# PEER expert stage: expert buffers of four slots by a quarter tile, added through four column groups of TensorE

## The reference, cut to what matters

```
s1, s2  = scores of the query's halves against 128 keys each
v1, i1  = top_k(s1, 16); v2, i2 = top_k(s2, 16)
w, p    = top_k(v1[:, None] + v2[None, :], 16)
expert  = i1[p // 16] * 128 + i2[p % 16]
y      += softmax(w) * gelu(dot(u[expert], h2)) @ v[expert]
```

## Time and profile before

| | |
|---|---|
| median of 3 runs | 1576.5 us (1575.19 to 1578.99) |
| profiled execution, its own time | 1576.8 us |
| its span, first to last instruction | 1575.5 us |
| mean granted clock of PE | 0.906 |
| busy: PE, DVE, ACT, POOL | 1310.1, 969.3, 283.7, 303.1 us |
| HBM read | 381.60 MB |

### The profile page before, as it was taken

How to read it: one execution, slowest core, us unless ns; L and a number is a source line. 1 busy time by engine, 2 the same in 40 slices (tenths; PEclk the granted TensorE clock), 3 DMA queues, 4 the chain that set the end, 5 groups by cost and what they waited for, 6 DMA issues and landing times.

```text
span 1575.5 us, 13461 instructions
## 1 busy us (share of the span) xinstructions
PE 1310.1 (83%) x4409; PEld 751.7 (48%) x4409; DVE 969.3 (62%) x2619; ACT 283.7 (18%) x642; POOL 303.1 (19%) x260
## 2 busy tenths in 40 slices
PE   7997999998899769998768739787878879696887
PEld 4766655676755336444454514333333435252333
DVE  5486533278453245541224789797969797888755
ACT  2014322102322211242221211111101010101000
POOL 0000000000000000000000044444544535354550
PEclk9998999999899769999658969898998989899999
DMA  7542453363153051053000199999999999999995
GB/s 280 189 148 107 160 173 137 107 218 143 54 214 107 32 195 56 32 208 142 1 0 1 61 415 426 425 426 424 426 424 427 423 415 424 419 418 415 422 427 244
DMA packets 105560, 384.58 MB, mean 244 GB/s; under 512 B 10763, under 2 KB 33854, under 8 KB 72722
## 3 DMA queue, kind: packets, MB, share of 16 engines
q0 software_dynamic: 36864, 268.45, 40.6%
q1 hardware_dynamic: 68626, 115.27, 20.6%
HBM read 381.60 MB, written 1.05 MB: 243 GB/s over the span
## 4 chain that ended last, share of the span: by engine, by line
PE 28%; DMA 17%; DVE 15%; issue 2%; ACT 2%; POOL 1%; DVEq 0%; SPq 0%; ACTq 0%
PE bank L174 27%; DMA e_uv<-in_experts_dram,e_chosen 17%; DVE e_uv L2459 3%; DVE e_hot L190 1%; DVE e_diag L196 1%; POOL e_uv L2583 1%; DVE second_hT L197 1%; DVE ml_W L190 1%; PE bank L179 1%; DVE e_e L215 1%; ACT m_sq L234 1%; DMA m_fin_g<-in_final_g_dram 0%; DVE m_fin_g L202 0%; ACT m_ctx L238 0%; DVE e_part L196 0%
## 5 line engine op out<-in xcount | busy, mean ns | idle before, releaser
L174 PE MATMUL bank<-e_uv,e_diag 128*128 128x512 f32 x1024 | 478.7, 625 | 133.7 <-DVE e_diag L196 133.6
L2583 POOL DMA_INDIRECT e_uv<-in_experts_dram,e_chosen x256 | 302.9, 1183 | 1231.7 <-DVE e_chosen L207 900.4
L174 PEld LDWEIGHTS bank<-e_uv,e_diag 128*128 128x128 f32 x1024 | 200.8, 200 | 400.5 <-issue 257.6
L2459 DVE CUSTOM_DVE_ANT_0 e_uv<-e_uv,second_h 128x1024 f32<-128x1024 f32 x256 | 305.0, 1222 | 99.5 <-DMA e_uv<-in_experts_dram,e_chosen 99.4
L174 PE MATMUL bank<-hT,weights 128*128 128x256 f32 x640 | 149.8, 397 | 10.4 <-DVE fb L202 8.8
L174 PEld LDWEIGHTS bank<-hT,weights 128*128 128x128 f32 x640 | 127.0, 200 | 29.7 <-DVE fb L202 8.9
L174 PE MATMUL bank<-weights,hT 128*128 128x512 f32 (+1 forms) x256 | 102.0, 555 | 2.0 <-DMA weights<-in_w_in_dram 2.0
L234 ACT ACTIVATE e_act<-e_dot 128x4 f32<-128x4 f32 (+1 forms) x67 | 13.7, 205 | 487.7 <-DVE e_dot L2459 487.7
L202 DVE SCALAR_TENSOR_TENSOR conv<-ubuf,vec,conv 128x256 f32<-128x256 f32 x240 | 96.8, 480 | 0.6
L174 PE MATMUL bank<-weights,mixT 128*128 128x512 f32 x192 | 91.1, 630 | 1.8 <-DVE mixT L207 1.6
L174 PE MATMUL bank<-m_w,second_hT 128*128 128x512 f32 (+1 forms) x160 | 70.3, 598 | 3.3 <-DVE second_hT L197 1.9
(11 more groups left out here) (350 smaller groups left out, 1326.3 us busy)
## 6 DMA issues: line engine op xcount, KB each, us to landing
weights<-in_w_in_dram SPq DMA_DIRECT2D x16, 2048.0 KB, 7.7
weights<-in_w_ada_dram SPq DMA_DIRECT2D x8, 2048.0 KB, 7.7
weights<-in_w_out_dram SPq DMA_DIRECT2D x6, 2048.0 KB, 7.6
weights<-in_cmp_w_dram SPq DMA_DIRECT2D x4, 2048.0 KB, 8.0
m_w<-in_w_ada_dram SPq DMA_DIRECT2D x4, 2048.0 KB, 8.3
e_w_pq<-in_w_pq_dram SPq DMA_DIRECT2D x8, 1024.0 KB, 24.4
m_w<-in_w_in_dram SPq DMA_DIRECT2D x3, 2048.0 KB, 14.0
m_w<-in_w_out_dram SPq DMA_DIRECT2D x2, 2048.0 KB, 8.7
```

The costliest lines, as they stand in the source:

```text
L174: ins = self.engine.matmul(out, lhsT, rhs, start=start, stop=stop, **kw)
L2459: dve.mark(c.nc.vector.tensor_tensor_reduce(u, u, h2[:, tt, :], 1.0, 0.0, MUL, ADD, m["dot"][:, j:j + 1]), ("dots_set", turn, b) if n == e ...
L2583: ins = c.nc.gpsimd.indirect_dma_start(out=m["uv"][j], out_offset=None, in_=A["experts"], in_offset=bass.IndirectOffsetOnAxis(ap=of, axis=0))
```

## The change: what it does

A buffer no longer holds one slot of 128 tokens. Its four groups of 32 partitions hold four slots (4m to 4m+3) of the same 32 tokens, a quarter of the tile; buffer `j` = 4m + q holds quarter q. Buffers, bytes and gathers stay 16, 1 MB and 256. What follows from it:

- `add`: the stationary matrix is 128x32 (the constant `fold`, four stacked 32x32 identities, times the weights) and sums the four slots; the product of buffer `j` goes to partitions 32q to 32q+31 of the bank, in column group q of PE. The four buffers of a batch follow each other, first for one half of the columns, then for the other. All four are released by one event, `uv_free{j // 4}`.
- `diags`: one DVE product of [128, 4, 32] in place of four of [128, 128].
- `h2q`: the dots need h2 as the buffers lie: quarter q four times under each other. PE makes it by products with the identity as moving operand (`quarter_turned`, 32 products for a quarter, eight quarters), in a ring of the four held banks, and ACT copies each half bank out (`quarter_set`). `hT`, `scores`, `cand`, `rest`, `hot` and `keysT` move to other memory to make room.
- expert numbers and weights are computed with a token on each partition, as before, and spread to the new layout by 16 small products each (`list_spread`, `weights_spread`). DVE copies the list to `listed` (event `list_set`, for which POOL now waits), ACT copies the weights (`weight_set`).
- `places` loses the cast to `chosen` and the sum for the softmax, which ACT's exp now leaves in `norm`.

The diff, cut to its core:

```diff
 def peer_tensor
+    def quarter_turned(tt, q):
+        tokens = slice(tt * P + q * SIDE, tt * P + q * SIDE + SIDE)
+        for half in range(2):
+            n = (tt * QUARTERS + q) * 2 + half
+            if n >= len(spare):
+                pe.wait_ge(*at("h2_set", n - len(spare)))
+            for k in range(4):
+                for s in range(QUARTERS):
+                    pe.mm(spare[n % len(spare)][s * SIDE:s * SIDE + SIDE, k * P:k * P + P], hT[:, 4 * half + k, tokens], ident,
+                          skip_group_check=True, tile_position=(0, s * SIDE),
+                          tell=("h2_turned", n) if (k, s) == (3, QUARTERS - 1) else None)
+    def spread(name, bank, src, turn, tt):
+        if turn or tt:
+            pe.wait_ge(*at(name + "_set", *divmod(turn * NT + tt - 1, NT)))
+        for q in range(QUARTERS):
+            for s in range(QUARTERS):
+                pe.mm(bank[SIDE * s:SIDE * s + SIDE, :, q], ident[:, q * SIDE:q * SIDE + SIDE], by_slot[:, :, s],
+                      skip_group_check=True, tile_position=(0, SIDE * s), ...)
     def add(turn, b):
         pe.wait_ge(*at("diags_set", turn, b))
-        for n in range(*batches_of(turn)[b]):
-            for h in range(2):
-                pe.mm(acc[tt][h], m["diag"][j], m["uv"][j][:, D + h * 512:D + h * 512 + 512], start=first, stop=last,
-                      skip_group_check=True, tell=(f"uv_free{j}", turn, tt) if h else None)
+        for h in range(2):
+            for n in range(n0, end):
+                pe.mm(acc[tt][h][g * SIDE:g * SIDE + SIDE, :], m["diag"][:, j, :], m["uv"][j][:, D + h * 512:D + h * 512 + 512],
+                      start=first, stop=last, skip_group_check=True, tile_position=(0, g * SIDE),
+                      tell=(f"uv_free{j // BATCH}", turn, tt) if h and g == QUARTERS - 1 else None)
...
-    for tt in range(NT):
-        h2_turned(tt)
+    for q in range(QUARTERS):
+        quarter_turned(0, q)
+        if q == 1:
+            list_spread(0, 0)
+    weights_spread(0, 0, 0)
+    for q in range(QUARTERS):
+        quarter_turned(1, q)
+    pe.wait_ge(*at("h2_set", 2 * NT * QUARTERS - 1))
     keys_turned(1)
     queries(1, 0)
     queries(1, 1)
     scores(1)
-    pe.wait_ge(*at("h2_set", NT - 1, 1))
+    list_spread(0, 1)
+    weights_spread(0, 1, 1)
 def peer_vector
+    def listed(head, tt):
+        dve.wait_ge(*at("list_spread", head, tt))
+        dve.copy(m["listed"][:, head % 2, tt], bank_l[:, 0:BUFS], tell=("list_set", head, tt))
     def diags(turn, b):
-        for j in range(j0, j1):
-            dve.ts(m["diag"][j], K["ident"], m["w"][:, j:j + 1], MUL, settled=False, ...)
+        dve.tt(m["diag"][:, j0:j1], wide(K["fold"].unsqueeze(1), shape), wide(m["w"][:, j0:j1].unsqueeze(2), shape), MUL,
+               tell=("diags_set", turn, b))
     for tt in range(NT):
         for step in ("halves", "candidates", "places"):
             route(0, tt, step)
-    dve.wait_ge(*at("h2_set", NT - 1, 1))
+        listed(0, tt)
 def peer_scalar
-    h2_turned(0)
-    soft(0, 0)
-    h2_turned(1)
-    soft(0, 1)
-    keys_turned(1)
-    queries(1)
-    scores(1)
+    for q in range(QUARTERS):
+        quarter_set(0, q)
+        if q == 1:
+            soft(0, 0)
+    weighted(0, 0)
+    for q in range(QUARTERS):
+        quarter_set(1, q)
+    keys_turned(1)
+    queries(1)
+    soft(0, 1)
+    scores(1)
+    weighted(0, 1)
 def peer_gpsimd
             if j == 0:
-                pool.wait_ge(*at("chosen_set", turn, tt))
+                pool.wait_ge(*at("list_set", turn, tt))
```

More of the change, by code:

```diff
@@ L1461, in mix_memory @@
     m["xn"] = m["h2"]
+    m["hT"], m["hT_ctx"] = (second["hT"][:, i * KT * T:(i + 1) * KT * T].rearrange("p (k t) -> p k t", k=KT) for i in range(2))
     m["w"] = [tile(f"w{i}", [P, 4096]) for i in range(3)]
@@ L2221 @@
 BUFS, BATCH = TOPK, 4
+QUARTERS = P // SIDE
 BATCHES = NT * TOPK // BATCH
@@ L2250, in peer_memory @@
     m["uv"] = uv + [tile(f"uv{j}", [P, 2 * D]) for j in range(2, BUFS)]
-    m["diag"] = [tile(f"diag{j}", [P, P]) for j in range(BUFS)]
+    more = tile("h2q", [P, 4, D])
+    left = second["hT"][:, KT * T:].rearrange("p (c d) -> p c d", c=2)
+    m["h2q"] = [[left[:, 0], left[:, 1], more[:, 0], more[:, 1]],
+                [more[:, 2], more[:, 3], second["h2"][:, 0], second["h2"][:, 1]]]
+    m["hT"] = second["hT"][:, 0:KT * T].rearrange("p (k t) -> p k t", k=KT)
+    m["scores"] = cond["mod_rows"].rearrange("p (t a k) -> p t a k", t=NT, a=2)
+    select = K["select"].rearrange("p (i n) -> p i n", i=4)
+    m["cand"], m["rest"], m["hot"] = select[:, 0], select[:, 1], select[:, 2].rearrange("p (i j) -> p i j", i=TOPK)
+    m["keysT"] = select[:, 3].rearrange("p (a k) -> p a k", a=2)
     for name, shape, dt in (
[L2253 to L2256, removed]
+            ("diag", [P, BUFS, SIDE], F32), ("dot", [P, BUFS], F32), ("act", [P, BUFS], F32), ("w", [P, BUFS], F32),
+            ("listed", [P, 2, NT, BUFS], U32), ("weight", [P, 2, NT, BUFS], F32), ("qT", [P, 2, T], F32),
+            ("sv", [P, NT, 2, TOPK], F32), ("si", [P, NT, 2, TOPK], U32), ("sif", [P, NT, 2, TOPK], F32),
             ("best", [P, NT, TOPK], F32), ("pos", [P, NT, TOPK], U32), ("part", [P, NT, TOPK], U32),
@@ L2333, in peer_tensor @@
-    for bank in range(3):
+        n0, end = batches_of(turn)[b]
+        tt = n0 // BUFS
+        for h in range(2):
+            for n in range(n0, end):
+                j = n % BUFS
+                g = j % QUARTERS
+                first, last = turn == 0 and j < QUARTERS, turn == PEER_H - 1 and j >= BUFS - QUARTERS
+                pe.mm(acc[tt][h][g * SIDE:g * SIDE + SIDE, :], m["diag"][:, j, :], m["uv"][j][:, D + h * 512:D + h * 512 + 512],
+                      start=first, stop=last, skip_group_check=True, tile_position=(0, g * SIDE),
+                      tell=(f"uv_free{j // BATCH}", turn, tt) if h and g == QUARTERS - 1 else None)
@@ L2334, in peer_tensor @@
+    spare = held
+    for bank in range(4):
         c.banks.leave(bank)
@@ L2357, in peer_tensor @@
                 scores(head)
+            if turn + 1 < PEER_H and b in ROUTE_AT and ROUTE_AT[b][1] == "places":
+                tt = ROUTE_AT[b][0]
+                list_spread(turn + 1, tt)
+                weights_spread(turn + 1, tt, min(turn + 1 + tt, PEER_H - 1))
             if b >= behind:
@@ L2531, in soft, with weighted @@
         act.wait_ge(*at("gap_set", head, tt))
-        act.f(m["best"][:, tt], m["gap"][:, tt], ACT.Exp, tell=("exp_set", head, tt))
+        act.f(m["best"][:, tt], m["gap"][:, tt], ACT.Exp, accum_out=m["norm"][:, tt:tt + 1], tell=("exp_set", head, tt))
+    def weighted(head, tt):
+        act.wait_ge(*at("weight_spread", head, tt))
+        if head >= 2:
+            act.wait_ge(*at("diags_set", head - 2, len(batches_of(head - 2)) // NT * (tt + 1) - 1))
+        act.copy(m["weight"][:, head % 2, tt], bank_k[:, 2 * P:2 * P + BUFS], tell=("weight_set", head, tt))
     def gelu(turn, b):
@@ L2570, in peer_scalar @@
                 soft(turn + 1, ROUTE_AT[b][0])
+            if turn + 1 < PEER_H and b in LISTED_AT:
+                weighted(turn + 1, LISTED_AT[b])
 def peer_gpsimd(c, m, A):
```

91 lines of the change are left out of this document (50 added, 41 removed).

## The result

The changed kernel takes 1577.92 us (median of 16 runs, 1576.85 to 1581.59), the kernel before 1575.64 (16 runs on the same chip). The ratio is **1.0017**, 95% interval 1.001 to 1.0025: slower by 1.6 to 3.9 us. The interval is clear of 1, and the difference is under the 0.2% that the forecast itself took as what can be measured. The profiled span is 1576.7 us against 1575.5. The forecast was 1586.

A forecast was written before the change was run, and what follows sets the result against it. The DMA stream was taken to bound the expert stage. A first gather 4.3 us late, idle DMA of 5.8 and 1.5, less 2.2 at the end, made +9.4 us: 1586 us, range 1576 to 1600.

The forecast's parts named there:

- the quick rival: Preparation on PE: records cost 0.028 us, first gather at 903.0, DMA queue never dry, total 1576.7 us; chance 0.18.
- The record's price: Small PE products before the first gather and first dot: 0.045 us a record, ranging from 0.035 to 0.057.
- The line through the wide-weight rows: Pricing PE's new records: 0.131 us at 128 weight columns and 0.075 at 64 carry on to 0.047 at 32.
- the proportion of the two column-group rows: Pricing PE's new records: 0.12 us at 512 moving columns and 0.057 at 256 would give 0.028 at 128.
- The first dot: DVE's first dot waits for the copy of tile 1's list: 933.8 against 913.30, 20.5 us late.
- The hole: DMA idle around the first buffers' return: 5.8 us from 950.5 to 956.3, then 1.5 us at the next four.
- the rule: Idle DMA runs from the queue's end, set by the first gather, to the refill, set by the first dot: 5.8 us.
- The second half: Later expert stage: after the early stalls nothing more is late, and the stream's rate stays unchanged.
- 11 us of queue: Expert stage: a gather takes at least 11 us from issue to landing, so earlier buffer release starts nothing earlier.
- The stream's rival: Expert stage: earlier release by PE closes DMA dips and returns 7.6 us, 1569 with quick records; chance 0.08.
- The end: After the last product PE has only four records left, 1.7 to 3.4 us: 2.2 us gained.
- No gain from PE: Expert stage: adds cost PE some 360 of its 479 us less, worth nothing while the DMA queue is full.

The follow-up runs named there:

- Lists early: Changed kernel with tile 1's list, exp and weights made before head 1's keys, queries and scores: median 1575.5 us, ratio 1.0005 to the kernel before.
- exp first: Changed kernel with ACT making tile 0's exp before it copies the quarters: 1578.07 us, ratio 1.0011 to the kernel before.
- the half adds: Kernel before, only the second half of v multiplied in routings 1 to 6: 1575.89 us; with gathers in fours 1577.59; with one of four diagonal products 1575.34.
- the kernel with unread products: Changed kernel with four more DVE products of 128x128 in each batch, written to a tile nobody reads: 1603.34 us, again 1603.43, ratio 1.0165.

## Why the prediction was right and wrong

The direction was right and the size four times too large: +9.4 us forecast, +2.3 measured in the medians, +1.2 in the two spans. By the forecast's own threshold of 3.2 us that is the same time. It lies within 2 us of the quick rival's 1576.7, but by luck: that rival has no hole and an unchanged stream, and here a hole of 4.9 us and a gain of 3.4 us in the stream nearly cancel. By the forecast's steps:

- **The record's price is the term that failed.** 0.045 us was taken and 0.029 measured (3.70/128), a spread's record 0.013 where 0.045 was taken too. The line through the wide-weight rows was the wrong guide; the proportion of the two column-group rows, 0.028, was right at 128 columns. The first gather came 2.6 us late, 2.2 by the change, not 4.3. In the forecast's own sum this price alone takes +9.4 to the quick rival's -0.1. The Trainium skill ("TensorE: Matmul & The Clock Gate", LDWEIGHTS) gave an estimated 0.027 for the load: it was the nearer price.
- **The first dot** was due at 933.8 and came at 929.19. At the measured price it would have been near 923.5, as the quick rival said. PE's two gaps, 5.1 us, brought it to nearly 929. The sum had no term for them, and that is its second failed step; two errors of opposite sign made the dot look nearly right. The gaps also took the quick rival down: it needed a queue that never ran dry.
- **The hole**: forecast 5.8 + 1.5 = 7.3 us of idle DMA, measured 4.9 by bytes. Place, cause and the half clock of the first add (3.64 us) were right. So was the rule: a first gather 1.7 us earlier than forecast and a first dot 4.6 us earlier make 7.3 + 1.7 - 4.6 = 4.4. Lists early showed the cause, exp first the step that a start alone is worth nothing while the hole is there.
- **The second half** was forecast as unchanged, by 11 us of queue, and gave back 3.4 us: the third failed step, a term put at nothing. From 970 to 1530 the mean rate rose from 422.4 to 425.0 GB/s, 0.6%, which is over the 0.5% that the forecast named as a sign of being wrong. The stream's rival had named the gain, at up to 7.6 us, but by PE's earlier release, which the half adds show to be insufficient by itself. Its size is shown, its cause stays open.
- **The end**: 2.2 forecast, 3.0 measured. The forecast had taken the middle of 1.7 and 3.4 us for the last four records, and they took 1.90, at full clock.
- **No gain from PE**: right as far as the half adds test it, for a lighter PE alone gained nothing clear of noise. An add of four is 1.9 to 3.6 us. The forecast of over 350 us less PE time was wrong: the adds lost 271, because the idler PE ran many of them at the lower clock (0.64 to 0.68 granted where it was 0.92 to 0.95), and the added products, with other records that the lower clock made longer, took 40 back. PE as a whole lost 231.7 us of busy time (the page's 1078.4 against 1310.1).

Put into the forecast's own sum: 2.6 + 4.9 - 3.4 - 3.0 = +1.1 in place of +9.4. Start and hole together are 4.1 of the difference: the price's 9.5, less some 5 that the gaps took back; the second half is 3.4, the end 0.8.

## What to carry to other kernels

Where a queue is full and sets the pace, don't count on relief of one engine (half the adds, or one product of four, gained nothing clear of noise here), and the price of a change is found in what it puts ahead of the first round: ask which copy the first consumer waits for, and place that work before anything that is only needed later. Check every `<-issue` gap in a stretch where DMA is saturated; a long run of small instructions beside it can lose as much as it takes (15.3 us idle in the kernel with unread products, where the 512 records of the quarters are 15.4 us of work in the changed kernel). Before times of two executions are compared, check how far apart they are at a point that the change doesn't touch (up to 3.6 us here). Price an unseen short form from rows of its own kind (same number of weight columns), not along a line through others.

## What the runs showed of the hardware that I had not expected

- PE loses time beside gathers, with nothing waited for that the profile shows: 5.7 us from 896 to 950 in the changed kernel and 15.3 in one with four more DVE products a batch; with the gathers held, 0.8 and 1.6. In the second kernel holding the gathers back by 22 us was a gain of 8. That its instructions come late is how I read it.
- Records with 32 weight columns in four column groups: 0.029 us at 128 moving columns, 0.013 at 4, where the transposes cost 1.91/16 = 0.12. An add of four is 1.92 us at full clock against 7, 3.6 times; in a single column group four records alone take 1.90.
- With the DMA share at 1.01 and gathers landing 10.5 us and more after their issue, the rate was 425 GB/s in one kernel and 419 in another over 260 us, and heavier DVE load took the first to 418 (landings of 9.7 us and more).
